# An expert's output rows scaled where they are stored and added to the residual by DMAs; VectorE's last two low pieces of the first expert unit moved up in the routing stage

## Chip, cores and metric

One core of a Trainium2 chip runs the whole program. The metric is device time in microseconds, the median of three runs; one more execution was recorded by the hardware profiler, and all rows below come from it.

## What is computed

Two layers of a decoder over 256 positions of width 1024 (batch 1). Layer 0 mixes tokens with a gated MLP and has a dense SwiGLU; layer 1 mixes with latent attention and has a SwiGLU with 8 experts, of which each position uses 2. Both mixers run beside a cross-attention into 256 memory tokens. The change touches the experts of layer 1 and the last norm:

```python
def moe_ffn(x, w_router, b_router, w_gate, w_up, w_down):
    logits = (x @ w_router).astype(jnp.float32) + b_router.astype(jnp.float32)
    top_vals, top_idx = lax.top_k(logits, TOP_K)
    weights = jax.nn.softmax(top_vals, axis=-1)
    gates = jnp.sum(jax.nn.one_hot(top_idx, N_EXPERTS, dtype=jnp.float32) * weights[..., None], axis=-2)
    out = jnp.zeros_like(x)
    for e in range(N_EXPERTS):
        out = out + gates[..., e:e + 1].astype(x.dtype) * swiglu(x, w_gate[e], w_up[e], w_down[e])
    return out
...
h = h + moe_ffn(rms_norm(h, ffn_norm[1]), ...)
return rms_norm(h, final_norm)
```

## The kernel before

**Numbers and tiles.** Every large product is made of float32 numbers split in two: a high part `hi` (ScalarE copies `raw` to it, line 1156) and a low part `lo` (VectorE subtracts, line 1606). TensorE then does three products for each block (lines 584, 585, 586: lo by hi, hi by lo, hi by hi). Weights come in units of 128 partitions by up to 3584 columns. There are three `raw` buffers and two of `hi` and `lo`, and a unit is split in four pieces. SyncE loads a unit's half into a `raw` buffer when VectorE has made the low parts of the unit that was there three units earlier (it waits on `lo_done`; helpers `load` and `expert_loads`, lines 513 and 519).

**The experts.** The program picks for every position its two experts (routing, some 490 to 510 us), then runs a loop over the experts, `ve` from 0 to 7 here (up to 16 rounds where an expert has over 128 positions). A round takes 12 units U+0 to U+11 of 896 or 1024 columns a piece: eight of gate and up weights, loaded at line 513, and four of down weights (line 519). Its 128 rows come from a table in HBM, `slots`, into which GpSimd has scattered the normalised rows by indirect DMAs (line 2322); expert 0 is fed from SBUF by a selection product instead. A round's output stays in the two PSUM banks S; at the start of the next round ScalarE copies them to `yrow` (`output_rows`, through line 1156), and SyncE stores `yrow` in block `ve` of `slots` after the loads of unit U+5 (line 524). After unit U+9's loads it fetches the next expert's rows, `xrow` (line 529). The output of the last round is never stored: it is split in high and low parts (`output_hi` on ScalarE, `output_lo` on VectorE, line 2104) and put on its positions by a selection product (`scatter`, line 1059).

**The routing stage on VectorE** is an order written out by hand: `add_tile`, `gain_tile`, `choose` (the top two of a tile's logits), `rows_lo`, `sel`, counts, and between them the four low pieces of unit U+0, by `split(U_MOE, 0, (i,))`. Pieces 0 and 1 stand inside the stage; piece 2 and piece 3 stand behind it, after each half of `gathered_lo` (line 2098, the low parts of the first expert's turned rows).

**The end.** When the outputs of the rounds before the last are stored, GpSimd gathers each position's two rows by four indirect DMAs, 512 KB each (line 2333), into `y_from[k][t]` (k is the choice, t the tile of 128 positions). VectorE multiplies each by its gate and adds it to the residual `h` (`add_rows`, line 2109), four times:

```python
            dve.wait_ge(gates_set, 1)
            dve.wait_ge(y_back, 16 * 2 * NT)
            for k in range(2):
                add_rows(k, 0)
            output_lo(0)
            add_rows(0, 1)
            output_lo(1)
            add_output(0, 0)
            add_output(0, 1)
            add_rows(1, 1)
            add_output(1, 0)
            add_output(1, 1)
```

`add_output(t, c)` (line 2116) adds the last expert's product for tile t and column half c. ScalarE squares each finished quarter (line 1585), GpSimd makes `rstd` of a tile from its two sums (lines 2339, 2341), VectorE and ScalarE scale (lines 2197, 1589), and SyncE stores the four quarters (line 546).

## Time and profile before

| | |
|---|---|
| median of 3 runs | 1008.78 us (1007.81 to 1008.89) |
| the profiled execution: its own time | 1007.8 us |
| its span, first to last instruction | 1006.0 us |
| TensorE busy | 982.1 us (98%), granted clock 0.997 of full speed |
| VectorE, ScalarE, GpSimd busy | 756.4 us (75%), 656.1 us (65%), 60.6 us (6%) |
| moved by DMAs | 287.12 MB, mean 285 GB/s |

Times are counted from the first instruction, so 992.8 is a place in the span and not a duration. In a timeline row the first number is the start, the second the busy time of the merged group, "x4" the number of instructions, and the bracket the idle time of that engine before it with what ended it. A row of a table by stretch gives the busy time of each engine with its count, then the granted clock, the mean busy share of the 16 DMA engines and what they moved. "PE" is TensorE, "DVE" VectorE, "ACT" ScalarE, "POOL" GpSimd, "SPq" SyncE's queue of DMA issues. In the profile's names `R` stands for R1, R2 and R3, in which xn, `yrow`, `xfirst` and three of the gathered tiles lie; the fourth lies in `GB` (GB1).

### The profile page before, as it was taken

The page shows a single profiled execution, that of the slowest core. Times are in us where ns is not written, and L with a number is a line of the kernel's source. Part 1 is how long each engine was busy: PE and PEld are TensorE (multiplying, and loading weights), DVE is VectorE, ACT ScalarE, POOL GpSimd, SP SyncE. Part 2 cuts the span into 40 slices and gives each one's busy share as a digit, 9 for nine tenths or more (in the row PEclk, how much of TensorE's full clock was granted, in tenths as well). Part 3 has the DMA queues.
Part 4 walks back from the last instruction along what each step waited for, and adds up shares of the span by engine and source line. Part 5 has one row for each costly group of instructions (what it writes and reads, how often), then busy time and mean ns, then how long its engine had stood idle before and what let it go on. Part 6 is the DMA issues. An engine that isn't in the chain of part 4 may idle for free.

```text
span 1006.0 us, 14574 instructions
## 1 busy us (share of the span) xinstructions
PE 982.1 (98%) x4892; PEld 829.4 (82%) x4892; DVE 756.4 (75%) x915; ACT 656.1 (65%) x886; POOL 60.6 (6%) x86
## 2 busy tenths in 40 slices
PE   8999999999999999999999999999999999999995
PEld 6987887888887998988877888888888888888883
DVE  5557665456556566666687989898998989899888
ACT  5555345452445545554596787978879787887964
POOL 1301000000000100000160000000000000000141
PEclk9999999999999999999999999999999999999998
DMA  9843689995566657233669999999999999999992
GB/s 322 237 156 128 189 250 309 289 319 156 200 202 216 220 149 190 103 124 106 219 226 400 399 384 407 378 402 371 390 374 385 406 371 401 373 387 391 381 405 101
DMA packets 150536, 287.12 MB, mean 285 GB/s; under 512 B 12769, under 2 KB 58865, under 8 KB 150498
## 3 DMA queue, kind: packets, MB, share of 16 engines
q1 hardware_dynamic: 147890, 277.64, 77.9%
q0 software_dynamic: 2608, 8.98, 2.6%
q8 instruction: 24, 0.39, 0.2%
q14 instruction: 14, 0.11, 0.0%
HBM read 269.81 MB, written 16.78 MB: 285 GB/s over the span
## 4 chain that ended last, share of the span: by engine, by line
PE 82%; DVE 8%; ACT 3%; DMA 3%; issue 2%; POOL 1%; SPq 1%; DVEq 0%; POOLq 0%; ACTq 0%
PE A L584 20%; PE A L586 20%; PE A L585 20%; PE S L584 4%; PE S L586 4%; PE S L585 4%; DVE lo L1606 3%; PE T L629 2%; DMA raw<-in_moe_w_down 1%; DMA raw<-in_moe_w_up 1%; PE T L1091 1%; ACT hi L1156 1%; PE T L664 1%; PE T L1049 1%; ACT R L1211 1%
## 5 line engine op out<-in xcount | busy, mean ns | idle before, releaser
L1606 DVE TENSOR_TENSOR lo<-raw,hi 128x1024 fp32r<-128x1024 f32 (+4 forms) x532 | 570.8, 1130 | 122.0 <-ACT hi L1156 120.0
L1156 ACT ACTIVATE hi<-raw 128x1024 fp32r<-128x1024 f32 (+4 forms) x532 | 485.2, 981 | 149.6 <-PE A L586 123.3
L584 PE MATMUL A<-lo,xT_hi 128*128 128x512 f32 x820 | 324.1, 395 | 2.5 <-DVE lo L1606 2.4
L586 PE MATMUL A<-hi,xT_hi 128*128 128x512 f32 x820 | 319.9, 390 | 0.0
L585 PE MATMUL A<-hi,xT_lo 128*128 128x512 f32 x820 | 319.6, 390 | 0.0
L584 PEld LDWEIGHTS A<-lo,xT_hi 128*128 128x128 f32 x820 | 154.3, 188 | 35.0 <-DVE lo L1606 3.2
L586 PEld LDWEIGHTS A<-hi,xT_hi 128*128 128x128 f32 x820 | 154.0, 188 | 32.3
L585 PEld LDWEIGHTS A<-hi,xT_lo 128*128 128x128 f32 x820 | 154.3, 188 | 30.2
L584 PE MATMUL S<-lo,xT_hi 128*128 128x512 f32 x224 | 89.1, 398 | 1.0 <-DVE lo L1606 1.0
L586 PE MATMUL S<-hi,xT_hi 128*128 128x512 f32 x224 | 87.5, 391 | 0.0
L585 PE MATMUL S<-hi,xT_lo 128*128 128x512 f32 x224 | 87.4, 390 | 0.0
L1156 ACT ACTIVATE xT_hi<-T 128x512 fp32r<-128x512 f32 (+1 forms) x82 | 41.6, 545 | 46.9 <-PE T L629 16.3
L584 PE MATMUL A<-lo,wk_hi 128*128 128x512 f32 (+2 forms) x152 | 56.9, 374 | 0.0
L586 PE MATMUL A<-hi,wk_hi 128*128 128x512 f32 (+2 forms) x152 | 56.3, 370 | 0.0
L585 PE MATMUL A<-hi,wk_lo 128*128 128x512 f32 (+2 forms) x152 | 56.2, 370 | 0.0
L584 PEld LDWEIGHTS S<-lo,xT_hi 128*128 128x128 f32 x224 | 42.2, 189 | 10.8 <-DVE lo L1606 2.7
L586 PEld LDWEIGHTS S<-hi,xT_hi 128*128 128x128 f32 x224 | 42.1, 188 | 8.8
L585 PEld LDWEIGHTS S<-hi,xT_lo 128*128 128x128 f32 x224 | 42.1, 188 | 8.1
L1637 DVE TENSOR_TENSOR xT_lo<-T,xT_hi 128x512 fp32r<-128x512 f32 (+1 forms) x34 | 19.6, 593 | 28.4 <-ACT xT_hi L1156 28.4
L584 PE MATMUL A<-xT_lo,hi 128*128 128x256 f32 x128 | 37.6, 294 | 0.4 <-DVE lo L1606 0.4
L629 PEld LDWEIGHTS T<-ident,R 128*128 128x128 f32 x228 | 27.4, 145 | 12.8 <-issue 4.5
L629 PE MATMUL T<-ident,R 128*128 128x128 f32 x228 | 33.4, 283 | 4.6 <-DVE R L1673 1.5
(239 smaller groups left out, 884.8 us busy)
## 6 DMA issues: line engine op xcount, KB each, us to landing
raw<-in_moe_w_down SPq DMA_DIRECT2D x64, 896.0 KB, 9.4
raw<-in_moe_w_gate SPq DMA_DIRECT2D x32, 768.0 KB, 8.0
raw<-in_moe_w_up SPq DMA_DIRECT2D x24, 768.0 KB, 7.3
raw<-in_moe_w_gate SPq DMA_DIRECT2D x16, 1024.0 KB, 6.9
raw<-in_moe_w_up SPq DMA_DIRECT2D x32, 512.0 KB, 6.8
raw<-in_moe_w_up SPq DMA_DIRECT2D x16, 1024.0 KB, 8.0
raw<-in_ff_w_gate SPq DMA_DIRECT2D x10, 1024.0 KB, 6.0
raw<-in_ff_w_up SPq DMA_DIRECT2D x10, 1024.0 KB, 7.2
```

Of the source, the lines that this page charges most:

```text
L584: nc.tensor.matmul(out, stat[0], mov[1], start=start, stop=False)
L585: nc.tensor.matmul(out, stat[1], mov[0], start=False, stop=False)
L586: return nc.tensor.matmul(out, stat[0], mov[0], start=False, stop=stop)
L629: last = nc.tensor.transpose(bank[:, i * P:(i + 1) * P], b, ident[:, :])
L664: last = nc.tensor.matmul(bank[:, i * P:(i + 1) * P], a.values[:, b, hd * P:(hd + 1) * P], PPT[:, (g - 1) % 2, at:at + P], start=b == 0, s ...
L1049: last = nc.tensor.transpose(T[j % 2][:, i * P:(i + 1) * P], xrow[:, (4 * b + i) * P:(4 * b + i + 1) * P], ident[:, :])
L1091: last = nc.tensor.transpose(T[j % 2][:, b * P:(b + 1) * P], hid[:, 4 * n + b, :], ident[:, :])
L1156: return nc.scalar.activation(out, in_, ACT.Copy)
L1211: last = nc.scalar.activation(PP[:, (g + 1) % 2, i * n:(i + 1) * n], S[gg % 2][:, i * n:(i + 1) * n], ACT.Exp, bias=nb[:, gg, i:i + 1], sc ...
L1606: nc.vector.tensor_tensor(piece(lo, SPLIT, u, i), piece(raw, RAW, u, i), piece(hi, SPLIT, u, i).bitcast(F32), ALU.subtract).then_inc(lo_do ...
L1637: nc.vector.tensor_tensor(out, T[j % 2][:, 0:n * P].rearrange("p (k s) -> p k s", k=n), hi_part.bitcast(F32), ALU.subtract).then_inc(t_fre ...
```

## The change

Four things, all in layer 1's experts:

1. **Gates as a table.** A second table in HBM, `gate_slots`, holds one gate per slot. SyncE zeroes it with one DMA, and the small tile `slot_gate` with another, ahead of the first zeroing of `slots`. After the scatter of the rows GpSimd scatters the gates by four more indirect DMAs (128 numbers each). After each round's `xrow` fetch SyncE fetches the next block's 128 gates into `slot_gate` (4 bytes to a partition), having waited once for the four scatters.
2. **Scaled where stored.** ScalarE's `output_rows` multiplies by `slot_gate` as it copies S to `yrow`, having waited for the fetch of the round before.
3. **Added by DMAs.** The four `add_rows` are gone from VectorE. GpSimd, once all four gathers have landed, issues two DMAs that add `y_from[0][t]` to `h[:, t, :]`, waits for both, and issues the two of choice 1. VectorE waits for all four (`added_in`) between `output_lo(0)` and the first `add_output`; the quarters now go c before t on VectorE and on ScalarE, and GpSimd's wait for tile 0 is for three squares in place of two.
4. **Low pieces moved.** Piece 2 of unit U+0 goes ahead of `choose(1)`, piece 3 ahead of the copy of `xfirst`.

```diff
@@ -247,6 +247,8 @@
     slot_rows = slots.rearrange("b p d -> (b p) d")
+    gate_slots = nc.dram_tensor("gate_slots", (BLOCKS * P, 1), F32, kind="Internal").ap()
+    gate_blocks = gate_slots.rearrange("(b p) o -> b p o", p=P)
@@ -333,6 +335,7 @@
         gate_row = sb("gate_row", [P, 2, NT])
+        slot_gate = sb("slot_gate", [P, 1])
         rowf = sb("rowf", [P, 2, 2, NT])
@@ -387,7 +390,8 @@
         gate_set, rows_added, tile_summed = sem("gate_set"), sem("rows_added"), sem("tile_summed")
-        gates_set = sem("gates_set")
+        gates_set, gates_in = sem("gates_set"), sem("gates_in")
+        slot_gate_in, added_in = sem("slot_gate_in"), sem("added_in")
         last_gained, last_out = sem("last_gained"), sem("last_out")
@@ -496,6 +500,11 @@
                     sp.wait_ge(zero_set, 1)
+                    if b == 0:
+                        zeros = sel[:, :].bitcast(F32)
+                        sp.dma_start(gate_slots.rearrange("(p b) o -> p (b o)", p=P), zeros[:, 0:BLOCKS]
+                                     ).then_inc(zero_in, 16)
+                        sp.dma_start(slot_gate[:, :], zeros[:, 0:1]).then_inc(slot_gate_in, 16)
                     sp.dma_start(slots[b].rearrange("p (a c) -> p a c", c=NT * P),
@@ -528,6 +537,9 @@
                                      ).then_inc(xrow_in, 16)
+                        sp.wait_ge(gates_in, 16 * 2 * NT)
+                        sp.dma_start(slot_gate[:, :], gate_blocks[bass.ds(ve + 1, 1)].rearrange("b p o -> p (b o)"),
+                                     allow_slow_non_contiguous=True).then_inc(slot_gate_in, 16)
@@ -1510,8 +1522,10 @@
                     act.wait_ge(y_stored, ve * 16 + 16)
-                act_copy(yrow[:, c * 512:(c + 1) * 512], S[(S_MOE + c) % 2][:, :]
-                         ).then_inc(s_free[(S_MOE + c) % 2], 1)
+                if c == 0:
+                    act.wait_ge(slot_gate_in, ve * 16 + 16)
+                nc.scalar.activation(yrow[:, c * 512:(c + 1) * 512], S[(S_MOE + c) % 2][:, :], ACT.Copy,
+                                     scale=slot_gate[:, 0:1]).then_inc(s_free[(S_MOE + c) % 2], 1)
@@ -1577,7 +1591,7 @@
             for n in range(4):
-                t, c = divmod(n, 2)
+                c, t = divmod(n, 2)
                 cols = slice(c * 512, (c + 1) * 512)
@@ -2067,7 +2081,7 @@
             gain_tile(1, 1)
-            split(U_MOE, 0, (1,))
+            split(U_MOE, 0, (1, 2))
             choose(1)
@@ -2086,6 +2100,7 @@
             nc.vector.tensor_tensor(r1[:, 2, :], top[:, :, 1], top[:, :, 0], ALU.subtract).then_inc(ahead_set, 1)
+            split(U_MOE, 0, (3,))
             dve.wait_ge(row_mm, 2)
@@ -2103,11 +2118,6 @@
                                         ALU.subtract).then_inc(y_lo, 1)
-
-            def add_rows(k, t):
-
-                step(nc.vector.scalar_tensor_tensor(h[:, t, :], y_from[k][t], gate_row[:, k, t:t + 1],
-                                                    h[:, t, :], ALU.mult, ALU.add))
@@ -2138,9 +2148,7 @@
             gathered_lo(T_MOE, 0, (0,))
-            split(U_MOE, 0, (2,))
             gathered_lo(T_MOE, 0, (1,))
-            split(U_MOE, 0, (3,))
             split(U_MOE + 1)
@@ -2174,17 +2182,12 @@
                     split(U + 1, ve + 1)
-            dve.wait_ge(gates_set, 1)
-            dve.wait_ge(y_back, 16 * 2 * NT)
-            for k in range(2):
-                add_rows(k, 0)
             output_lo(0)
-            add_rows(0, 1)
+            dve.wait_ge(added_in, 16 * 2 * NT)
+            add_output(0, 0)
             output_lo(1)
-            add_output(0, 0)
+            add_output(1, 0)
             add_output(0, 1)
-            add_rows(1, 1)
-            add_output(1, 0)
             add_output(1, 1)
@@ -2313,7 +2316,7 @@
             nc.gpsimd.tensor_scalar(rowf[:, 1], rowf[:, 0], r1[:, 8, 1:2], None, ALU.is_lt).then_inc(row_to_set, 1)
-            pool.wait_ge(zero_in, 16 * (BLOCKS - 1))
+            pool.wait_ge(zero_in, 16 * BLOCKS)
             pool.wait_ge(y_stored, 16)
@@ -2323,6 +2326,11 @@
             nc.gpsimd.tensor_tensor(gate_row[:, :, :], rowf[:, 1], r1[:, 5:7, :], ALU.mult).then_inc(gates_set, 1)
+            pool.wait_ge(gates_set, 1)
+            for k in range(2):
+                for t in range(NT):
+                    pool.indirect_dma_start(gate_slots, bass.IndirectOffsetOnAxis(row_to[:, k, t:t + 1], 0),
+                                            gate_row[:, k, t:t + 1], None).then_inc(gates_in, 16)
             pool.wait_ge(route_done, 1)
@@ -2333,9 +2341,15 @@
                                             ).then_inc(y_back, 16)
+            pool.wait_ge(y_back, 16 * 2 * NT)
+            for k in range(2):
+                if k:
+                    pool.wait_ge(added_in, 16 * NT)
+                for t in range(NT):
+                    pool.dma_start(h[:, t, :], y_from[k][t], accum_op=ALU.add).then_inc(added_in, 16)
             n = N_FINAL
             for t in range(NT):
-                pool.wait_ge(tile_summed, 2 * t + 2)
+                pool.wait_ge(tile_summed, t + 3)
                 step(nc.gpsimd.tensor_scalar(rstd[:, n, t:t + 1], half_sum[:, t, 0:1], half_sum[:, t, 1:2], EPS,
```

How the order moves, in three places.

VectorE, behind the routing stage and ahead of the loop over the experts, before:

```order
L2086 COPY ahead<-A 128x8 x2
L2088 TENSOR_TENSOR r<-top 128x2
L2090 COPY R<-S 128x512
L2098 TENSOR_TENSOR xT_lo<-T,xT_hi 128x512
L1606 TENSOR_TENSOR lo<-raw,hi 128x1024
L2098 TENSOR_TENSOR xT_lo<-T,xT_hi 128x512
L1606 TENSOR_TENSOR lo<-raw,hi 128x512
L1606 TENSOR_TENSOR lo<-raw,hi 128x1024 x3
L1606 TENSOR_TENSOR lo<-raw,hi 128x512
```

and with the change:

```order
L2100 COPY ahead<-A 128x8 x2
L2102 TENSOR_TENSOR r<-top 128x2
L1620 TENSOR_TENSOR lo<-raw,hi 128x512
L2105 COPY R<-S 128x512
L2113 TENSOR_TENSOR xT_lo<-T,xT_hi 128x512 x2
L1620 TENSOR_TENSOR lo<-raw,hi 128x1024 x3
L1620 TENSOR_TENSOR lo<-raw,hi 128x512
```

The piece of 512 columns (piece 3) has moved ahead of the copy of `xfirst`; the piece of 1024 (piece 2) has left this stretch and stands further up, beside piece 1. Both low parts of the turned rows now follow each other.

VectorE behind the loop, before:

```order
L2109 SCALAR_TENSOR_TENSOR h<-R,gate_row,h 128x1024 x2
L2104 TENSOR_TENSOR wk_lo<-S,wk_hi 128x512
L2109 SCALAR_TENSOR_TENSOR h<-R,gate_row,h 128x1024
L2104 TENSOR_TENSOR wk_lo<-S,wk_hi 128x512
L2116 SCALAR_TENSOR_TENSOR h<-A,gate_last,h 128x512 x2
L2109 SCALAR_TENSOR_TENSOR h<-GB,gate_row,h 128x1024
L2116 SCALAR_TENSOR_TENSOR h<-A,gate_last,h 128x512 x2
```

and with the change:

```order
L2119 TENSOR_TENSOR wk_lo<-S,wk_hi 128x512
L2126 SCALAR_TENSOR_TENSOR h<-A,gate_last,h 128x512
L2119 TENSOR_TENSOR wk_lo<-S,wk_hi 128x512
L2126 SCALAR_TENSOR_TENSOR h<-A,gate_last,h 128x512 x3
L2194 TENSOR_TENSOR R<-h,GB 128x512
```

The four rows of 1024 columns are gone, and the second `wk_lo` (`output_lo(1)`) now stands behind the first `add_output` and so behind the wait for the adding DMAs.

GpSimd from the scatter of the rows on, with the change (line 2332 and line 2349 are new):

```order
L2325 DMA slots<-R,row_to 2304x1024 x4
L2328 TENSOR_TENSOR gate_row<-rowf,r 128x4
L2332 DMA gate_slots<-gate_row,row_to 2304x1 x4
L2335 TENSOR_LOAD nround
L2335 ISA x2
L2337 ISA
L2338 TENSOR_TENSOR row_from<-row_to,row_kept 128x4
L2341 DMA R<-slots,row_from 128x1024 x3
L2341 DMA GB<-slots,row_from 128x1024
L2349 DMA h<-R 128x1024 x3
L2349 DMA h<-GB 128x1024
L2353 TENSOR_SCALAR rstd<-half_sum 128x1
```

The gate scatters stand behind the row scatters, the adding DMAs behind the gathers; nothing else moved there.

## Rows read from the trace of the kernel before

**Rows 1.** Table by stretch: PE, PEld, DVE, ACT, POOL busy, PEclk, DMA share, GB/s

```profile
508.00:513.00 5.00, 4.63 (x24) 3.46 (x23) 4.29 (x6) 3.92 (x7) 4.37 (x9) 1.00 0.01 2
521.00:527.00 6.00, 6.00 (x28) 4.94 (x27) 6.00 (x8) 5.52 (x7) 5.09 (x4) 1.00 0.93 288
527.00:534.00 7.00, 7.00 (x32) 5.82 (x31) 6.76 (x7) 4.27 (x7) 0.34 (x2) 1.00 1.03 414
600.00:700.00 100.00, 100.00 (x464) 83.55 (x463) 90.81 (x98) 81.69 (x104) 0.00 (x0) 1.00 1.03 389
```

**Rows 2.** Timeline of TensorE: where it stood still in the first round

```profile
546.95 0.50 PE L584 MATMUL A<-lo,xT_hi 128*128 128x512 f32 x1 [1.89 <-DVE lo L1606]
...
552.49 0.50 PE L584 MATMUL S<-lo,xT_hi 128*128 128x512 f32 x1 [0.48 <-DVE lo L1606]
```

**Rows 3.** Timelines of SyncE's queue (DMA issues) and of GpSimd, first round

```profile
512.60 0.37 SPq L513 DMA_DIRECT2D raw<-in_moe_w_up  x1
...
521.31 0.37 SPq L513 DMA_DIRECT2D raw<-in_moe_w_gate  x1
...
527.13 0.22 POOL L2325 TENSOR_TENSOR gate_row<-rowf,r 128x4 f32<-128x4 f32 x1
...
543.60 0.33 SPq L529 DMA_DIRECT2D R<-slots  x1
548.06 7.87 SPq L519 DMA_DIRECT2D raw<-in_moe_w_down  x4
```

**Rows 4.** Timelines of ScalarE (first row) and VectorE in and behind routing

```profile
498.31 2.00 ACT L1156 ACTIVATE hi<-raw 128x1024 fp32r<-128x1024 f32 x2
...
501.25 1.22 DVE L1606 TENSOR_TENSOR lo<-raw,hi 128x1024 fp32r<-128x1024 f32 x1
503.49 0.23 DVE L2048 SCALAR_TENSOR_TENSOR rt<-A,rstd,br 128x8 f32<-128x8 f32 x1 [1.02 <-PE A L968]
...
508.33 0.69 DVE L2090 COPY R<-S 128x512 f32<-128x512 f32 x1 [0.92 <-PE S L1031]
...
511.74 4.81 DVE L1606 TENSOR_TENSOR lo<-raw,hi 128x512 fp32r<-128x512 f32 x5
```

**Rows 5.** DMA view of 28 to 41 us, then of 98 to 104 us: issue, KB, us to landing

```profile
gbs<-in_gm_b_s POOLq DMA_DIRECT2D x1, 4.0 KB, 5.8
...
GB<-in_mem_norm POOLq DMA_DIRECT2D x1, 512.0 KB, 4.0
```

**Rows 6.** GpSimd's last gather, then the DMA view of 962 to 977 us

```profile
965.51 1.96 POOL L2333 DMA_INDIRECT GB<-slots,row_from  x1 [0.30 <-issue]
...
q0 software_dynamic: 576, 2.10, 35.4%
...
GB<-slots,row_from POOLq DMA_INDIRECT x1, 11.4
```

**Rows 7.** Timeline of the last two weight units: TensorE, ScalarE, VectorE

```profile
982.42 0.50 PE L584 MATMUL S<-lo,xT_hi 128*128 128x512 f32 x1 [0.47 <-DVE lo L1606]
...
984.67 1.79 ACT L1156 ACTIVATE hi<-raw 128x896 fp32r<-128x896 f32 x2 [0.46 <-DMA raw<-in_moe_w_down]
986.71 1.79 ACT L1156 ACTIVATE hi<-raw 128x896 fp32r<-128x896 f32 x2 [0.24 <-DMA raw<-in_moe_w_down]
...
985.66 4.13 DVE L1606 TENSOR_TENSOR lo<-raw,hi 128x896 fp32r<-128x896 f32 x4 [0.16 <-ACT hi L1156]
```

**Rows 8.** Timelines of the end: TensorE, VectorE, GpSimd

```profile
992.45 0.39 PE L586 MATMUL S<-hi,xT_hi 128*128 128x512 f32 x1
...
992.34 0.69 DVE L2104 TENSOR_TENSOR wk_lo<-S,wk_hi 128x512 fp32r<-128x512 f32 x1
...
996.51 1.27 DVE L2109 SCALAR_TENSOR_TENSOR h<-GB,gate_row,h 128x1024 f32<-128x1024 f32 x1
997.82 1.41 DVE L2116 SCALAR_TENSOR_TENSOR h<-A,gate_last,h 128x512 f32<-128x512 f32 x2
...
1002.12 0.75 DVE L2197 SCALAR_TENSOR_TENSOR R<-h,rstd,GB 128x512 f32<-128x512 f32 x1 [0.77 <-POOL rstd L2341]
...
1000.23 1.20 POOL L2339 TENSOR_SCALAR rstd<-half_sum 128x1 f32<-128x1 f32 x1 [1.61 <-ACT R L1585]
```

## The prediction

> **What bounds the kernel now.** I read the chain of waits first: TensorE carries most of it. The table by stretch [rows 1] says where that is strict. From 600 to 700 us TensorE is busy for all 100 us, and the DMAs carry 389 GB/s. In other stretches they reach 414 GB/s, so in the middle rounds TensorE alone sets the pace and a weight that comes a little earlier or later is worth nothing. That leaves three places where time can be won or lost.
>
> The first is the first round. The DMAs stand still from 508 to 513 us (2 GB/s) and run at 288 GB/s from 521 to 527, since SyncE waits to be allowed to load: the second half of unit U+3 is issued at 512.60, the first half of U+5 at 521.31 [rows 3], each when VectorE has made the low parts three units back. The bill comes at 546.95, where TensorE waits 1.89 us for low parts whose weights were late, and at 552.49, 0.48 us more [rows 2]. The second is the last two weight units, where TensorE waits again (0.47 us) and ScalarE starts each of the last halves when its DMA lands, at 984.67 and 986.71 [rows 7]: here the DMAs set the end. The third is the end itself: the last product of the experts finishes at 992.45 + 0.39 = 992.84 [rows 8], and from there to the end of the span, 1006.0, are 13.2 us of short steps, mostly VectorE's.
>
> **The low pieces moved up.** Piece 2 has had its high part since 498.31 + 2.00 = 500.31 [rows 4]. VectorE makes piece 1 at 501.25 in 1.22 us and then idles 1.02 us until the logits of tile 1. A second piece of up to 1.22 us ends at 503.69 at the latest, against 503.49 for the start of `choose(1)`; the issue overlaps by some 0.1 us, so the routing chain is **0.1 us** later, at most 0.2, at least 0. Piece 3, half a piece, fits in the 0.92 us idle before the copy of `xfirst` at 508.33. So the second half of U+3 can be issued some 4 us earlier, in the time when the DMAs stand still.
>
> What is behind it gains less. The five pieces that VectorE makes from 511.74 in 4.81 us [rows 4] become four. They can't start before their high parts, so I take U+1 and U+2 to be 1.3 us earlier, the load of U+5 with them, and from U+3 on, where ScalarE sets the pace, some 0.6 us. From 527 on the DMAs are full, so what counts is how much of the unused capacity before is recovered: (1 - 288/414) x 6 = 1.8 us between 521 and 527 [rows 1], of which loads issued 0.6 to 1.3 us earlier recover about 1. Forecast: **-1.0 us**; bounds: nothing, and both stalls, 1.89 + 0.48 = -2.4.
>
> **The gates' table.** GpSimd issues four more indirect DMAs behind 527.13 + 0.22 [rows 3]. It has nothing else to do until the gathers. They have to be in before SyncE's first fetch of gates, behind the row fetch at 543.60; the next issue there comes at 548.06 only, so 16 us and 4 more cover them. As to DMA time, the nearest row is the load of 1024 separate numbers, 5.8 us from issue to landing with other transfers beside it [rows 5]; 512 numbers are at most half of that, 2.9, in the window where the DMAs are the bound, and at least nothing. The landing holds mostly waiting, so I take 0.3. The fetches, 128 numbers each, are hidden in the middle rounds under a full TensorE; the one in the last round stands ahead of the last weights and I give it 0.1 (at most 5.8/8 = 0.7). Together **+0.4 us**, between 0 and 3.6. ScalarE's copies scaled by a column, the two zeroing DMAs and ScalarE's new wait (for a fetch issued a third of a round before) I take at nothing: TensorE's full busy time covers them.
>
> **The end without the four additions.** The four `add_rows` take 1.27 us each [rows 8]; two lie before the first `output_lo` at 992.34 and cost nothing, two lie between it and the last `add_output`, which ends at 997.82 + 1.41 = 999.23. With the change, from 992.84: the first scatter product of a tile 0.8 (estimate from four matmuls at 0.4 each, overlapped, as at the last one [rows 8]), one `add_output` 0.7, `output_lo(1)` 0.69, the second scatter 0.75, two `add_output` 1.41 give 997.2. That is 2.0 us less. GpSimd now makes tile 0's rstd right ahead of tile 1's (1.20 us for the first step at 1000.23), which may give back 0.2. What follows (square, rstd, scale, store) is the same. **-1.8 us**; bounds: -2.6 (both additions whole) and nothing.
>
> **The adding DMAs.** This is the term that decides. The last gather is issued at 965.51 and lands 11.4 us later, at 976.9 [rows 6]. GpSimd then issues two transfers of 512 KB. A plain one from GpSimd took 4.0 us from issue to landing with little beside it [rows 5], of which the data can be only about 1.3 at 400 GB/s, so the first bytes move some 2 us behind the issue, about 979.5. From there to 984.6, when the second-last half of the weights lands for ScalarE's start at 984.67, and 2 us beyond, the weights are still coming [rows 7], and both queues share the DMA engines. Their price: the four gathers, 2.10 MB, took 35.4% of the engines for 15 us, 5.3 us in all [rows 6]; two of them are 2.65. That is the cost if an adding transfer costs a copy. But it has to read `h` as well as its source; if reading is what limits, it is double, 5.3. I take the middle, 4.0. All of it fits ahead of the last weights and pushes them back. The slack there: VectorE's last four pieces end at 985.66 + 4.13 = 989.8 and three products of three matmuls (2.05 us by 0.23 each) end at 992.84, so 1.0; for the piece before, which five products follow, 0.6. So TensorE's end is 4.0 - 0.6 = **+3.4 us**; bounds 2.05 and 4.7. Nothing at all is excluded since the DMAs are full until the last weight.
>
> The second pair is issued when the first has landed. Sharing with the some 5.1 us of weights left, the first is in at 979.5 + 5.1 + 4.0 = 988.6, the second 4.0 + 3.3 (issue, first bytes, landing) later, 995.9. VectorE's first `add_output` is ready for it at 992.84 + 0.8 + 3.4 = 997.0. So `added_in` does not end last, by 1.1 us.
>
> **Sum.** +0.1 - 1.0 + 0.4 - 1.8 + 3.4 = **+1.1 us**. The profiled execution took 1007.8 us, so 1008.9 beside it; the median shown is 1008.78, 1.0 above that execution, so I predict **1009.9 us**. A measurement of this kernel tells about 0.2%, 2 us, from no change: this is inside.
>
> **Rivals.**
>
> *Two reads, half the rate.* The pair costs 5.3 us, the term 4.7, the sum -2.3 + 4.7 = +2.4: 1011.2 us. For it: the destination must be read. Against: the DMA engines' rate in these rows may be that of writing. The Trainium skill ("Collectives: The Full Stack", section "The bandwidth ceiling: the fold count and why AG ≠ RS ≠ AR") says that a transfer that adds puts two source reads on one ring and so runs at half the rate of a copy. By that rule this rival is right; no row before shows an adding transfer.
>
> *The wait takes the place of the additions.* If an adding transfer is cut small and costs three times a copy, a pair is 8.0 us. TensorE ends 7.4 later. The first pair is in at 979.5 + 5.1 + 8.0 = 992.6, the second 8.0 + 3.3 later, 1003.9, while VectorE stands ready at 993.6 + 7.4 = 1001.0 and `output_lo(1)` is queued behind that wait. Sum: -2.3 for the other terms, + 7.4 + 2.9 = +8.0, so 1016.8 us. It decides from a pair of about 5.1 us up. For it: the order puts the wait ahead of `output_lo(1)`. Against: the gathers ran at the full rate.
>
> *Faster.* The pair costs a copy (+2.05), the early half unit takes away all of the first round's stall (-2.4), the gates cost nothing: 0.1 - 2.4 - 1.8 + 2.05 = -2.05, so 1006.7 us. For it: 4 us of standing DMAs is more than the stall. Against: the later loads are not earlier by as much.
>
> **How the numbers follow.** Forecast 0.42, two reads 0.22, the wait 0.13, faster 0.23. The forecast lies within 2 us of before; two reads and the wait lie above; so 0.23 faster, 0.42 the same, 0.35 slower. The forecast's own range is 1008 to 1011. The whole range must reach both sides: down to the faster case with a full gain at the end (-2.6 instead of -1.8), 1005.9, and up to between two reads and the wait, 1015.0; beyond lie about 2 in 10.
>
> **What the profile would show.** The stall at 546.95 about 1 us shorter; the DMAs moving between 508 and 513; GpSimd's queue moving some 1 MB between 979 and 989; the last weights landing 4 us behind 986.7, seen as ScalarE waiting for them; `add_output` released by TensorE and not by a DMA; the stretch from the last expert product to the end at 11.4 us, not 13.2. I am wrong if an adding packet takes a copy's time, if `added_in` releases VectorE, or if the first stall does not shrink.

## The result, and the profile after

| | before | after |
|---|---|---|
| median of 4 runs each | 1008.32 us | 1018.65 us |
| lowest to highest | 1007.81 to 1008.89 | 1016.63 to 1020.38 |
| ratio, 95% interval | | 1.0102, 1.0081 to 1.0122 |
| the profiled execution, its span | 1007.8, 1006.0 us | 1016.63, 1014.9 us |

(A fourth run of the kernel before is in here, so its median is 1008.32 and not the 1008.78 of three.) The kernel is slower by 1.0%, 10.3 us between the medians and 8.9 us between the profiled spans. I had predicted 1009.9, range 1005.9 to 1015.0, slower with a chance of 0.35: the time lies outside the range.

Both kernels give TensorE the same 4892 matmuls in the same order, so their starts can be laid side by side. How much later each starts than in the kernel before, at eight places named by their time there:

```
                       routing  first round      middle    last weights      end
place, us before     508.1  540.1  552.5   600   975  |  982.4  989.2  992.5  span
after                +0.9   +5.2   +5.1   +5.0  +5.0  |  +4.4   +9.0   +9.1   +8.9
```

So 0.9 us come from routing, 4.1 from the first round (5.0 - 0.9), none from the middle, 4.1 from the last weights (9.1 - 5.0), and the end gives back 0.2.

**Routing.** VectorE and GpSimd in the kernel after, the timeline from 501 us:

```profile
501.22 2.35 DVE L1620 TENSOR_TENSOR lo<-raw,hi 128x1024 fp32r<-128x1024 f32 x2
504.34 0.23 DVE L2062 SCALAR_TENSOR_TENSOR rt<-A,rstd,br 128x8 f32<-128x8 f32 x1 [0.76 <-POOL rstd L2288]
...
501.51 2.15 POOL L2286 TENSOR_SCALAR rstd<-half_sum 128x1 f32<-128x1 f32 x1 [5.87 <-ACT R L1476]
503.74 0.56 POOL L2288 TENSOR_TENSOR rstd<-rstd,mhalf 128x1 f32<-128x1 f32 x1
```

`choose(1)` is 0.85 us later than in [rows 4], and not because VectorE is late: it has 0.76 us idle. It waits for GpSimd's rstd of tile 1. GpSimd's first step, one number to a partition, took 2.15 us and ended at 503.66, just when VectorE's two pieces ended (503.57).

**First round.** The table by stretch, columns as in [rows 1], of the kernel after, and under it the same two stretches of the kernel before:

```profile
534.00:538.00 4.00, 3.96 (x18) 2.96 (x16) 0.95 (x2) 1.58 (x2) 0.00 (x0) 1.00 1.04 121
538.00:544.00 6.00, 3.47 (x16) 2.40 (x16) 1.71 (x4) 1.10 (x2) 0.00 (x0) 1.00 0.93 226
544.00:550.00 6.00, 4.73 (x14) 3.79 (x15) 4.18 (x4) 4.18 (x7) 0.00 (x0) 0.72 1.06 364
```

```profile
534.00:538.00 4.00, 4.00 (x19) 3.31 (x18) 2.43 (x3) 1.90 (x3) 0.00 (x0) 1.00 1.04 402
538.00:544.00 6.00, 6.00 (x32) 5.01 (x31) 4.10 (x4) 4.57 (x7) 0.00 (x0) 1.00 1.11 358
```

The DMA engines are almost as busy as before and move far less: 121 GB/s for 402, then 226 for 358. GpSimd had issued the gates' scatters just before. Its timeline, and TensorE's stall that answers to [rows 2]:

```profile
525.94 1.66 POOL L2332 DMA_INDIRECT gate_slots<-gate_row,row_to  x1 [0.28 <-POOL gate_row L2328]
...
532.48 1.43 POOL L2332 DMA_INDIRECT gate_slots<-gate_row,row_to  x1 [0.30 <-issue]
...
545.27 0.50 PE L596 MATMUL A<-lo,xT_hi 128*128 128x512 f32 x1 [3.01 <-DVE lo L1620]
```

The stall is 3.0 us and stands 21 matmuls earlier in the program than the one of 1.89 us before. ScalarE waits 5.14 us for one load of up-weights at 542.90. After TensorE has stood still its clock is granted at 0.72 from 544 to 550, so part of that stretch runs at the lower of the two levels, 1.2 GHz in place of 2.4. Run 4 comes back to this.

The load I had looked at did come earlier: SyncE issues the second half of U+3 at 509.08, not 512.60 [rows 3].

**Last weights and end.** ScalarE, then VectorE in the kernel after, answering to [rows 7, 8]:

```profile
984.68 1.79 ACT L1168 ACTIVATE hi<-raw 128x896 fp32r<-128x896 f32 x2 [1.56 <-DMA raw<-in_moe_w_down]
986.82 1.80 ACT L1168 ACTIVATE hi<-raw 128x896 fp32r<-128x896 f32 x2 [0.34 <-DMA raw<-in_moe_w_down]
991.44 1.79 ACT L1168 ACTIVATE hi<-raw 128x896 fp32r<-128x896 f32 x2 [2.83 <-DMA raw<-in_moe_w_down]
996.15 1.79 ACT L1168 ACTIVATE hi<-raw 128x896 fp32r<-128x896 f32 x2 [2.92 <-DMA raw<-in_moe_w_down]
...
1002.02 0.60 ACT L1168 ACTIVATE wk_hi<-S 128x512 fp32r<-128x512 f32 x1 [0.76 <-PE S L598]
```

```profile
1001.29 0.69 DVE L2119 TENSOR_TENSOR wk_lo<-S,wk_hi 128x512 fp32r<-128x512 f32 x1 [2.06 <-ACT wk_hi L1168]
1003.72 0.75 DVE L2126 SCALAR_TENSOR_TENSOR h<-A,gate_last,h 128x512 f32<-128x512 f32 x1 [1.74 <-DMA h<-GB]
1004.38 0.68 DVE L2119 TENSOR_TENSOR wk_lo<-S,wk_hi 128x512 fp32r<-128x512 f32 x1
```

The last two half-units, which landed for ScalarE at 984.67 and 986.71 before, are in at 991.4 and 996.1: 9.4 us behind, of which 5.0 were there already. And at 1003.72 VectorE has waited 1.74 us for a DMA, the last of the four that add, with `output_lo(1)` queued behind that wait.

I measure the end from ScalarE's second copy of the experts' output (992.88 before; 1002.02 here) to the end of the span: 13.1 us before, 12.9 now.

### The profile page after: what moved, and what is told of

Same layout as the page of the kernel before. It is cut to its first block, busy times and chain, and to the rows that moved or that the text cites. A ratio compares the mean times of both kernels' runs of the same rounds, so it can differ in the third digit from the quotient of the medians.

```text
span 1014.9 us, 14609 instructions
## 1 busy us (share of the span) xinstructions
PE 985.7 (97%) x4892; PEld 830.4 (82%) x4892; DVE 752.0 (74%) x911; ACT 657.7 (65%) x886; POOL 70.6 (7%) x94
## 4 chain that ended last, share of the span: by engine, by line
PE 78%; DVE 6%; DMA 6%; ACT 4%; POOL 2%; issue 2%; SPq 1%; ACTq 0%; POOLq 0%; DVEq 0%
PE A L596 19%; PE A L598 19%; PE A L597 19%; PE S L596 4%; PE S L598 4%; PE S L597 4%; PE T L641 2%; DVE lo L1620 2%; DMA raw<-in_moe_w_up 2%; ACT hi L1168 2%; DMA h<-R 1%; DMA GB<-slots,row_from 1%; PE T L1103 1%; PE T L676 1%; DMA slots<-R 1%
```

## The experiments

The theory going in was that budget: GpSimd held up beside VectorE's second piece (+0.9), 4-byte writes that hold up all DMAs (+4.2), adding transfers at twice a copy's price ahead of the last weights (+4.6 from the dip at 982.4, 4.1 from the middle), and a wait that eats the gain of the end. The rivals were that the earlier load had upset the first round, and that two queues that share the engines cost the end its time whatever they carry. The shifts of TensorE in every run, read in the same way; the columns behind the bar are differences:

```
place, us before        508.1  552.5    600   975   992.5 | first  last     end,
                                                          | round  weights  us
after                    +0.9   +5.1   +5.0  +5.0   +9.1  | +4.1   +4.1    12.9
1  pieces alone          +1.1   +0.5   +0.5  +0.5   +1.2  | -0.6   +0.8    13.2
2  no adding DMAs        +0.7   +5.3   +5.2  +5.3   +4.9  | +4.6   -0.4    12.9
3  no gate scatters      +0.8   -1.5   -1.5  -1.5   +5.2  | -2.4   +6.8    12.0
4  plain copies          +1.5   +7.2   +7.1  +7.1   +9.8  | +5.6   +2.6    12.1
5  512 B rows            +0.8   +2.6   +2.6  +2.6   +7.7  | +1.8   +5.1    11.7
6  4 B, 512 B apart      +0.8   +0.6   +0.5  +0.5   +5.5  | -0.3   +4.9    12.2
7  4 B, 64 B apart       +0.6   +0.6   +0.5  +0.5   +7.2  | -0.1   +6.7    11.6
8  wait later            +3.1   +6.6   +6.6  +6.6  +10.6  | +3.5   +4.0    11.8
9  64 B, wait later      +1.1   +0.9   +0.9  +0.9   +7.7  | -0.2   +6.8    11.5
10 64 B, adds last       +0.9   -0.2   -0.3  -0.3   -0.7  | -1.2   -0.4    21.3
11 adding gathers        +0.6   +0.4   +0.3  +0.3   +4.7  | -0.3   +4.4    12.1
12 GpSimd adds, no table +1.2   +1.1   +1.1  +1.2   +5.9  |  0.0   +4.7    11.1
13 earlier add, no table +1.0   -0.3   -0.4  -0.4   +1.2  | -1.4   +1.5    12.4
14 one piece alone       +0.2   +0.5   +0.4  +0.4   -0.6  | +0.2   -1.0    13.2
```

("first round" is 600 less 508.1, "last weights" 992.5 less 975, "end" from the second copy to the end of the span.) Rows 1 and 12 to 14 are the kernel before with parts of the change or with other additions. One profiled execution each: routing alone scatters by some tenths of a us, once by 2 (row 8, where the granted clock was 0.73 from 508 to 513 us and 1.00 in the change).

### 1. The pieces alone

```diff
 (kernel before)
-            split(U_MOE, 0, (1,))
+            split(U_MOE, 0, (1, 2))
             choose(1)
...
+            split(U_MOE, 0, (3,))
             dve.wait_ge(row_mm, 2)
```

> The kernel before with the two moved low pieces alone. Theory (the budget read from the two traces: routing +0.9, gates' scatters +4.2, adding transfers +4.6, the wait eats the gain of the end): routing comes out 0.9 us later, because GpSimd's first step of tile 1's rstd stands still while VectorE makes two pieces (2.15 us instead of 1.10); the stall at 546.95 shrinks by up to 1 us since the second half of U+3 is loaded 4 us earlier; sum -0.1 to +0.9 us, so 1008.7 to 1009.7. Rival (the first round's delay comes from the earlier load, which changes the order of the loads): TensorE 4 to 5 us late after 550, 1013 to 1014 us.

Measured: 1008.20 us against 1008.84, ratio 0.9991 (0.9982 to 0.9999), 0.5 us under the expected range. The first round is not slower but 0.6 us faster than routing leaves it, and the interval just excludes no gain. The rival, 1013 us, falls.

### 2. The rows added by VectorE again

```diff
 (kernel after)
-            for k in range(2):
-                if k:
-                    pool.wait_ge(added_in, 16 * NT)
-                for t in range(NT):
-                    pool.dma_start(h[:, t, :], y_from[k][t], accum_op=ALU.add).then_inc(added_in, 16)
...
+                step(nc.vector.tensor_tensor(h[:, t, :], y_from[k][t], h[:, t, :], ALU.add))
```

> The changed kernel, its rows still scaled where stored, but added by VectorE in the places of the kernel before (plain additions), no adding DMAs. Theory: +0.9 of routing and +4.2 of the gates' scatters stay, the 4.6 on the last weights go, the end takes 13.2 us as before: 1008.8 + 5.1 = 1013.9 us, 1013.2 to 1014.5. Rival (the late last weights come from something else than the adding transfers, such as the fetch of gates ahead of them): above 1016 us.

Measured: 1013.80 us, ratio 1.0060 (1.0043 to 1.0077), the first round +4.6, the last weights -0.4. So the table of gates costs 5.6 us over the pieces alone, and the adding DMAs with all they change at the end 1018.65 - 1013.8 = 4.9.

### 3. No scatters of gates

> The changed kernel without the four scatters of gates (the table stays zero and the experts' rows of the first two choices come out as zeros: they are left out of the output); the fetches, the scaled copies and the adding DMAs stay. Theory: the DMAs keep 360 to 400 GB/s between 534 and 544 us and the first round's 4.2 us are gone: 1018.65 - 4.2 = 1014.4 us, 1013.7 to 1015. Rival (the pieces, or the zeroing of the table, cost the first round its time): 1018 us or more.

The edit takes out the loop of four `indirect_dma_start` into `gate_slots` and SyncE's wait for it. Measured: 1011.83 us, ratio 1.0033 (1.0020 to 1.0046): 6.8 us less than the change, more than the 4.2 expected and 1.9 under the range. This kernel's table stays zero, so the stored experts' rows are left out of its output; every step except the scatters is made. The stretches that stood at 121 and 226 GB/s:

```profile
534.00:538.00 4.00, 4.00 (x20) 3.30 (x19) 2.61 (x4) 1.76 (x3) 0.00 (x0) 1.00 1.05 402
538.00:544.00 6.00, 6.00 (x31) 5.13 (x30) 4.13 (x5) 5.63 (x9) 0.00 (x0) 1.00 1.11 359
```

Without the scatters the first round is 2.4 us faster than routing leaves it, so they cost not 4.1 but the gain of the pieces on top. How much that gain is, one trace doesn't tell: with both pieces moved and no scatters it is 0.6, 2.4, 0.0 and 1.4 us (rows 1, 3, 12, 13). Run 2 less run 1 makes it 5.2 in the first round and 5.6 in the time. The zeroing of the table and the fetches are still in here and cost nothing that shows.

At the end this run shows something that the change's own trace does not. Its table by stretch:

```profile
985.00:990.00 5.00, 3.46 (x16) 2.24 (x14) 2.09 (x2) 1.79 (x2) 0.05 (x1) 0.99 0.69 174
990.00:995.00 5.00, 3.20 (x8) 2.13 (x7) 2.09 (x2) 2.06 (x3) 1.65 (x2) 0.50 0.77 146
```

TensorE waited for the late weights and then ran at a granted clock of 0.50, the lower level; the products between 989 and 992.5 of the kernel before slip by 2.1 us. The last weights cost 6.8 us here for 4.1 in the change. Runs 5, 7 and 9 show the same (0.66, 0.66 and 0.50 between 995 and 1000 us; 1.7 to 2.8 us more from 989 to 992.5), runs 6 and 8 and the change itself do not (0.1). In run 11 it falls too, a little earlier in the program (0.91 from 985 to 990 us, 0.75 from 990 to 995).

### 4. The adding DMAs as plain copies

```diff
-                    pool.dma_start(h[:, t, :], y_from[k][t], accum_op=ALU.add).then_inc(added_in, 16)
+                    pool.dma_start(h[:, t, :], y_from[k][t]).then_inc(added_in, 16)
```

> The changed kernel with the four adding DMAs made plain copies of the same rows to the same places (the additions are left out of the output, h is overwritten). Theory (adding reads two operands and takes twice a copy's time): packets of that queue fall from 327 to 340 ns to about 160 to 170, the pair costs 2.65 us instead of 5.3, the last weights come 2.6 us earlier, the second pair is in before VectorE wants it, and the end gives its 1.8: 1018.65 - 4.4 = 1014.3 us, 1013.5 to 1016. Rival (two queues that share the DMA engines cost this, whatever they carry): 1018 us or more, packets above 300 ns.

Measured: 1016.24 us, ratio 1.0077 (1.0062 to 1.0092): 2.4 us less, not 4.4, and 0.2 above the range. Its first round was the worst of all (+5.6). The two stretches behind the scatters, of this run and then of run 8, which has the same packed table, differ in the granted clock:

```profile
538.00:544.00 6.00, 0.95 (x4) 0.53 (x3) 1.66 (x2) 1.58 (x2) 0.00 (x0) 0.74 1.00 214
544.00:550.00 6.00, 5.66 (x20) 4.35 (x20) 3.03 (x4) 3.25 (x4) 0.00 (x0) 0.69 0.95 294
```

```profile
538.00:544.00 6.00, 4.77 (x23) 3.43 (x23) 3.28 (x4) 1.58 (x2) 0.00 (x0) 1.00 1.01 219
544.00:550.00 6.00, 4.70 (x22) 3.55 (x21) 4.18 (x4) 4.94 (x7) 0.00 (x0) 1.00 1.02 329
```

With this table the first round costs 3.5 us where the clock stayed at 1.00 (run 8), 4.1 and 4.6 where it fell for a while (the change: 0.72 from 544 to 550; run 2: 0.82, then 0.89) and 5.6 where it fell longest. So part of this term may be the clock behind the stall, and not the late weights alone. The split is not tested: run 8 also came out of routing 2 us later, and in run 4 the DMAs were slower as well (294 GB/s from 544 to 550 for 329).

The end decides between the theories. GpSimd's queue in the DMA view while the second pair is alone, in the change (997 to 1004 us) and then here (996 to 1001 us):

```profile
q0 software_dynamic: 288, 1.05, 79.3%
...
h<-GB POOLq DMA_DIRECT2D x1, 512.0 KB, 6.6
```

```profile
q0 software_dynamic: 288, 1.05, 53.0%
...
h<-GB POOLq DMA_DIRECT2D x1, 512.0 KB, 3.7
```

The same 1.05 MB in 288 packets take 79.3% of 7 us, 5.55 us of all engines, when they add, and 53.0% of 5 us, 2.65 us, when they copy: a factor of 2.1. The last weights cost 2.6 us instead of 4.1. VectorE does not wait for a DMA, and the end takes 12.1 us:

```profile
1001.90 0.69 DVE L2119 TENSOR_TENSOR wk_lo<-S,wk_hi 128x512 fp32r<-128x512 f32 x1 [2.05 <-ACT wk_hi L1168]
1003.55 0.75 DVE L2126 SCALAR_TENSOR_TENSOR h<-A,gate_last,h 128x512 f32<-128x512 f32 x1 [0.96 <-PE A L1071]
...
1005.78 1.41 DVE L2126 SCALAR_TENSOR_TENSOR h<-A,gate_last,h 128x512 f32<-128x512 f32 x2 [0.22 <-PE A L1071]
1007.29 0.69 DVE L2194 TENSOR_TENSOR R<-h,GB 128x512 f32<-128x512 f32 x1
1008.93 1.41 DVE L2200 SCALAR_TENSOR_TENSOR R<-h,rstd,GB 128x512 f32<-128x512 f32 x2 [0.94 <-POOL rstd L2355]
```

This is the end without the four additions and without the wait: the last `add_output` ends 4.6 us behind ScalarE's second copy (1002.63), 6.35 before, so 1.8 are gained. But the rstd of both tiles now comes behind it. VectorE idles 0.94 us ahead of its first two scalings, where it went straight on before, and 0.46 for 0.77 [rows 8] ahead of the last: 0.7 go back.

### 5 to 7. What makes the scatters slow

Three tables in place of the one of 4 B per slot: 512 B per slot and written whole (with a constant, so its output is not the right one); 4 B written into rows of 512 B; 4 B written into rows of 64 B. The core of the second (the third has 16 for P):

```diff
-    gate_slots = nc.dram_tensor("gate_slots", (BLOCKS * P, 1), F32, kind="Internal").ap()
+    gate_slots = nc.dram_tensor("gate_slots", (BLOCKS * P, P), F32, kind="Internal").ap()
...
+            step(nc.gpsimd.tensor_scalar(row_far[:, :, :], rowf[:, 0], float(P), float(P * P), ALU.mult, ALU.add))
...
-                    pool.indirect_dma_start(gate_slots, bass.IndirectOffsetOnAxis(row_to[:, k, t:t + 1], 0),
+                    pool.indirect_dma_start(gate_slots.rearrange("b (o n) -> (b o) n", n=1), bass.IndirectOffsetOnAxis(row_far[:, k, t:t + 1], 0),
```

> The changed kernel with a table of 512 B for each slot, written whole by the same four scatters (rows of a constant, so what is scaled is not what the gates ask for). Theory (the four scatters hold the DMAs up because each of their 512 writes is 4 B into the same few KB): with 512 B rows a write is whole and 0.26 MB cost under 1 us; the DMAs keep above 350 GB/s between 534 and 544 us; the first round loses under 1.5 us instead of 4 to 7, the time is 1012.5 to 1014 us. Rival (the number of descriptors costs it, whatever their size): nothing changes, 1018 us or more, and the rate falls to 120 to 230 GB/s as before.

> The changed kernel with its numbers of 4 B written 512 B apart (a table 128 numbers wide, first column alone); one GpSimd step of 0.3 us more for the indices. Tells apart two readings of the slow scatters. Writes close together hit one place of the memory: spread, they cost under 1.5 us, 1012.5 to 1014 us. Writes of 4 B are slow wherever they go: 1018 us or more, the rate 120 to 230 GB/s between 534 and 544.

> As the table spread to 512 B between numbers, but 64 B (16 numbers wide). If what slows the 4 B writes is that several lie within one small block of memory (64 B or less), they cost under 1.5 us here too: 1012 to 1013.5 us. If they must lie hundreds of bytes apart, the rate between 534 and 544 us still falls below 300 GB/s and the time is 1014 to 1018.

Measured: 512 B rows 1013.80 us, ratio 1.0043 (1.0028 to 1.0058); 4 B in rows of 512 B 1012.43, ratio 1.0036 (1.0024 to 1.0048); 4 B in rows of 64 B 1012.91, ratio 1.0043 (1.0028 to 1.0059). The stretches of the second and the third:

```profile
534.00:538.00 4.00, 3.84 (x17) 2.84 (x16) 1.03 (x2) 1.58 (x2) 0.00 (x0) 1.00 1.04 398
538.00:544.00 6.00, 5.07 (x23) 3.71 (x24) 4.41 (x6) 3.82 (x5) 0.00 (x0) 1.00 1.11 361
```

```profile
534.00:538.00 4.00, 3.68 (x17) 2.71 (x15) 0.91 (x1) 1.58 (x2) 0.00 (x0) 1.00 1.04 382
538.00:544.00 6.00, 5.10 (x23) 3.78 (x24) 4.43 (x6) 3.91 (x5) 0.00 (x0) 1.00 1.11 362
```

With the same 512 writes of 4 B, by the same four DMAs, the first round is 0.1 to 1.2 us faster than routing leaves it when they lie 64 or 512 B apart (rows 6, 7, 9, 10 and 11), and 3.5 to 5.6 slower when 16 of them share 64 B; without any it is 0.0 to 2.4 faster. What spread writes still cost is not clear of the scatter between traces. Whole rows of 512 B cost more, +1.8 in their one trace, with the rate at 407 and 369 GB/s in the same two stretches. So the larger part goes with how the numbers are packed, not with their size or number. Wider spacing also makes the table larger, 9 KB at 4 B per slot and 147 KB at 64 B, and no run parts the two: whether it is neighbours in one block of 64 B, or all writes in a few KB, stays open. Which distance below 64 B would do was not tried, nor what in the memory makes it so. The Trainium skill ("DMA: Bandwidth & Descriptors", section "Specifications") says that a transfer of less than 512 B is done by reading, changing and writing back. That alone would make runs 6 and 7 as slow as the change, 1018 us, for their writes are 4 B too; the measured 1012.4 and 1012.9 decide against it as the whole cause.

### 8. The wait behind the second output_lo

```diff
             output_lo(0)
-            dve.wait_ge(added_in, 16 * 2 * NT)
-            add_output(0, 0)
             output_lo(1)
+            dve.wait_ge(added_in, 16 * 2 * NT)
+            add_output(0, 0)
```

> The changed kernel with VectorE's wait for the adding DMAs behind the second output_lo instead of ahead of it. Theory (the wait of 1.74 us holds output_lo(1) up, and the scatter of the second half behind it): output_lo(1) at 1002.7 instead of 1004.4, the end 0.7 to 1.0 us earlier: 1017.8 us. Rival (the first add_output alone decides): 1018.6, no change.

Measured: 1015.76 us, ratio 1.0071 (1.0048 to 1.0093), 2.9 less than the change, but the four runs lie between 1014.4 and 1019.3. In the trace the end takes 11.8 us for 12.9, and the wait that is left is 0.23 us. That is 1.1, a little over the 0.7 to 1.0 expected; the rest of the 2.9 I don't claim.

### 9 and 10. Closing the sum, and the additions behind the weights

> The changed kernel with both its avoidable costs taken off: numbers 64 B apart, and the wait for the adding DMAs behind the second output_lo. If the parts add up as read so far (pieces -0.6, scatters spread and fetches about +0.7, adding DMAs on the last weights +4.6, the end -1.1): 1008.8 + 3.6 = 1012.4 us less the share of the wait, 1011.5 to 1012.5. Rival (the parts overlap, something else of the change costs): above 1013.5 us.

> As the one with numbers 64 B apart and the later wait, but GpSimd issues the adding DMAs only when ScalarE has made the high part of the last weights' second-last piece, so that all weights are in. Theory (the 4.6 us are bytes ahead of the last weights, nothing else): the last weights land when they do in the kernel before, TensorE's last expert product ends 4 to 5 us earlier; but the two pairs, one behind the other, take 6.6 + 7.1 us from there (about 988 + 13.7 = 1001.7) and end 5 to 6 us behind the moment VectorE is ready: 1011.5 to 1012.5 us, about the same. Rival (the adding packets hold up more than their own time, so that moved behind the weights they cost less): below 1010.5 us.

The second of them adds, ahead of GpSimd's wait for the gathers:

```diff
+            pool.wait_ge(hi_done, n_pieces(U_MOE + 11, rounds - 1) + 3)
+            step(nc.gpsimd.tensor_tensor(r1[:, 8, 0:1], r1[:, 7, 1:2], r1[:, 7, 1:2], ALU.mult))
             pool.wait_ge(y_back, 16 * 2 * NT)
```

Measured: 1013.76 us, ratio 1.0051 (1.0034 to 1.0068), and 1016.19, ratio 1.0081 (1.0060 to 1.0101). The first is 1.3 us above the range I expected and 0.3 above the line set for the rival: with 6.8 us on the last weights it is among those whose clock fell, to 0.50. The second misses by 3.7. The weights are back in their place (TensorE 0.7 us early), but VectorE stands:

```profile
1003.19 2.73 DVE L2127 SCALAR_TENSOR_TENSOR h<-A,gate_last,h 128x512 f32<-128x512 f32 x4 [9.71 <-DMA h<-GB]
```

I had the first pair issued at 988.0 (it was 988.49), gave the pairs 13.7 us (14.7) and mis-added what follows. Two pairs in a row, alone, are a chain of 14.7 us, of which the moving itself is 2 x 5.55. Ahead of the weights they cost bytes, behind them their whole latency, which is worse.

### 11. Gathers that add

```diff
-                    pool.indirect_dma_start(y_from[k][t], None, slot_rows,
-                                            bass.IndirectOffsetOnAxis(row_from[:, k, t:t + 1], 0)
-                                            ).then_inc(y_back, 16)
+                    if k and not t:
+                        pool.wait_ge(added_in, 16 * NT)
+                    pool.indirect_dma_start(h[:, t, :], None, slot_rows,
+                                            bass.IndirectOffsetOnAxis(row_from[:, k, t:t + 1], 0),
+                                            compute_op=ALU.add).then_inc(added_in, 16)
```

> The changed kernel with the spread table, and with the gathers themselves adding to h (the first choice's two, then, when they are in, the second choice's two) in place of gathers and adding DMAs. Theory (an adding packet costs twice a copy's, and only half as many bytes move as with gathers and adding DMAs): the queue's share falls from 10.6 + 5.3 us of engine time to 10.6 in all; the last weights land 2.6 us later than in the kernel before instead of 4.6 to 7, no wait for the sums at the end, which takes 12.0 us instead of 13.1: about 1008.9 + 2.6 - 1.1 + 0.0 = 1010 to 1011 us. Rival (adding rows of an indirect DMA costs more than twice a copy): above 1012.4 us.

Measured: 1011.24 us, ratio 1.0026 (1.0006 to 1.0046). Of the versions with a table of gates it is the fastest, and still no faster than the kernel before. The DMA view of the stretch with its four gathers (958 to 991 us), and of the kernel before with its four (958 to 978):

```profile
q0 software_dynamic: 576, 2.10, 31.9%
```

```profile
q0 software_dynamic: 576, 2.10, 26.6%
```

10.5 us of engine time for 2.10 MB, against 5.3: twice again. My expectation had these 10.6 right and then put the last weights 2.6 late; the difference to the kernel before is 5.3, and they came 4.4 us late, in a trace in which the clock fell too (see run 3). The time lies 0.2 above the expected range.

### Two ways to take work from the end without DMAs

These are rows 12 and 13 of the table, and one piece alone is row 14. GpSimd scales and adds tile 1's rows (four operations), on the kernel before with the two pieces moved:

> The kernel before with the two moved low pieces and tile 1's rows scaled and added by GpSimd (four operations of 128x1024, from about 978 us, when the gathers are in) in place of two of VectorE's additions. Theory: GpSimd waits while VectorE makes pieces, so each takes 1 to 3 us and they are in by 990; both additions leave the stretch behind the last expert product: 1008.2 - 2.5 = 1005.7 us. Rival (GpSimd's operations hold VectorE's pieces up, or are themselves held up to the last piece and end behind 997): 1008 us or more.

Measured: 1010.00 us, ratio 1.0012 (1.0002 to 1.0021), so 1.8 slower than without. GpSimd and VectorE in that kernel:

```profile
978.45 3.15 POOL L2336 TENSOR_SCALAR R<-R,gate_row 128x1024 f32<-128x1024 f32 x1 [10.89 <-DMA GB<-slots,row_from]
981.70 3.04 POOL L2336 TENSOR_SCALAR GB<-GB,gate_row 128x1024 f32<-128x1024 f32 x1
984.82 2.97 POOL L2337 TENSOR_TENSOR h<-R,h 128x1024 f32<-128x1024 f32 x1
987.86 3.11 POOL L2338 TENSOR_TENSOR h<-GB,h 128x1024 f32<-128x1024 f32 x1
...
983.43 12.50 DVE L1606 TENSOR_TENSOR lo<-raw,hi 128x896 fp32r<-128x896 f32 x8 [0.35 <-ACT hi L1156]
```

The theory had GpSimd's times right (3.0 to 3.15 us each, in by 991), and the rival still won. VectorE's eight pieces took 1.56 us each in place of 1.03 (4.13 / 4 in [rows 7]): the last weights came 4.7 us late where the pieces alone have 0.8, and the end gained 2.1 (11.1 us for 13.2).

VectorE's addition of the first choice to tile 1, ahead of its last eight pieces:

```diff
                 with dve.If(ve < rounds - 1):
+                    split(U + 10, ve)
+                    split(U + 11, ve)
...
+            add_rows(0, 1)
+            split(U + 10, rounds - 1)
+            split(U + 11, rounds - 1)
             for k in range(2):
                 add_rows(k, 0)
             output_lo(0)
-            add_rows(0, 1)
             output_lo(1)
```

> The kernel before with the two moved low pieces, and in the last round VectorE's addition of the first choice's rows to tile 1 ahead of its last eight pieces (from about 981 us, where it idled 0.5 us and the gathers are in since 977) instead of between the two output_lo; the pieces of U+10 and U+11 stand behind the loop for that. Theory: the last pieces end 0.6 to 0.8 us later, of which TensorE has slack for most, and VectorE, which is busy without a break from the last expert product to the last add_output, loses 1.28 us there: 1008.2 - 0.8 = 1007.4 us, 1006.8 to 1007.8. Rival (the last pieces have no slack: what the addition takes there it takes in full): 1008.2 to 1008.8.

Measured: 1007.59 us against 1008.85, ratio 0.9987 (0.9978 to 0.9996). It beats both kernels, by 0.13% over the one before; its lead over the pieces alone is within their intervals. The trace shows both halves of the theory: the end takes 12.4 us for 13.2, and the last weights come 1.5 us late for 0.8.

One piece alone, moved to behind `choose(1)`:

> The kernel before with piece 2 alone moved, to just ahead of the copy of xfirst (1.22 us of work in 0.92 us of idle time) and piece 3 left behind the second gathered_lo. Theory (routing came 0.6 to 0.9 us late because GpSimd's first step of rstd waits for VectorE's two pieces): routing is as before up to 507 us, the GpSimd step takes 1.1 us, xfirst is 0.3 us late, U+3's second half is issued about 1 us earlier: 1008.0 us, within 0.5 of the two moved pieces. Rival (the gain of the moved pieces needs the 4 us earlier load): 1008.8 us.

Measured: 1008.34 us against 1008.85, ratio 0.9999 (0.9989 to 1.0008); by time it can't be told from either. The mechanism can. GpSimd's first step of rstd:

```profile
501.69 1.09 POOL L2283 TENSOR_SCALAR rstd<-half_sum 128x1 f32<-128x1 f32 x1 [5.87 <-ACT R L1464]
```

1.09 us with one piece beside it, 2.15 with two, and TensorE at 508.1 is 0.2 us late where every run with both pieces is 0.6 to 1.5 us late (and one 3.1).

## Why the prediction was wrong, by its own steps

**The low pieces, +0.1 and -1.0.** Together -0.9; alone they gave -0.6 in the time. The sum held, partly by luck: the parts were not as told. "The issue overlaps by some 0.1 us" left out GpSimd: I asked when VectorE would be free and not who works beside it. The Trainium skill ("SBUF — State Buffer", section "SBUF: two separate sides") has the rule that I should have weighed: a VectorE operation with two inputs in SBUF and a GpSimd operation that reads SBUF exclude each other for the whole instruction. The trace agrees, 1.09 us with one piece and 2.15 with two. Routing was 0.9 late. The first round gave 0.0 to 2.4 us back in four traces, where I had 1.0. In the changed kernel none of the gain was left, for the next term lay on the same stretch.

**The gates' table, +0.4, between 0 and 3.6. This is the step that failed.** It cost 5.6 us over the pieces alone (run 2 less run 1), outside its own bounds. That the scatters land in time was right, and that the fetches and the zeroing are hidden too (runs 2 and 3 have them; the last weights of run 2 are 0.4 early). What was wrong is the price of the DMA time. I took as upper bound a load of 1024 separate numbers, "512 numbers are at most half of that". That row is a read into SBUF; the change writes 4 B numbers side by side into HBM, and what it costs is not their own packets' time but that of the weights beside them, which fell to 121 GB/s. Nothing in the trace before shows such a write, so a row that was only near in size could not bound it. Runs 5 to 7 show that the packing sets most of it. This step alone puts the time outside the range: by estimate 1018.65 - (5.6 - 0.4) = 1013.4 us would have been inside, and the runs with spread numbers (1012.4 to 1013.8 us with the weights behind the adding DMAs) are.

**The adding DMAs, +3.4, between 2.05 and 4.7.** +4.1 in the change's trace, inside its bounds, between my 3.4 and the rival's 4.7. Of the seven traces with these DMAs ahead of the last weights (4.0 to 6.8 us) five lie above 4.7. The price of a pair was mine to choose between 2.65 and 5.3, and I took 4.0; alone it measures 5.55. The rival "Two reads, half the rate" was right in the rate; no run here shows that the second read is the reason. The Trainium skill ("Collectives: The Full Stack", section "The bandwidth ceiling: the fold count and why AG ≠ RS ≠ AR") states half a copy's rate for the reducing step of a collective, and the trace agrees for these DMAs, 5.55 us for 2.65. The first bytes moved later than I had them: the rate in the DMA view falls from about 420 to 300 GB/s at 986, 4 us behind the issue at 982.1 where I had taken 2. What no term held is the clock: where TensorE waited for such weights it was granted 0.50 for a while afterwards in four of the seven traces, and the last weights then cost 5.1 to 6.8 (4.0 to 4.9 in the others). The changed kernel's profiled execution escaped it at the end; I can't show whether its three longer runs (mean granted clock 0.990 to 0.993, for 0.994) did.

**The end, -1.8.** Run 4 shows it whole: 1.8 us are gained up to the last `add_output` and 0.7 given back behind it, where I had forecast 0.2, because both tiles' rstd now come behind the last `add_output`. In the change the wait took a further 0.8 to 0.9, so that 0.2 was left.

**"`added_in` does not end last, by 1.1 us."** Wrong by 2.8: it ended last by 1.74. The second pair landed at 997.10 + 6.6 = 1003.7. The rival "The wait takes the place of the additions" put its threshold at a pair of about 5.1 us, and the pair is 5.55, so it held in kind, with 1.7 us of wait and not 2.9. Its total of 1016.8 is close to the time, but for another reason: it has 7.4 us on the last weights and nothing in the first round.

**The sum.** By the trace +0.9 + 4.1 + 4.1 - 0.2 = 8.9. I had put these terms at +1.1. Of the 7.8 between, 4.7 are the first round's (the gates, and the gain of the pieces that they hid), 1.6 the end's, 0.8 routing's and 0.7 the adding DMAs'. The medians are 10.3 apart and not 8.9 because the profiled execution of the change was the fastest of its four, 2.0 under its median, and that of the kernel before 0.5 under its own. The medians of the runs give the same picture: -0.6 for the pieces, 5.6 for the table, where I had 0.4, and 4.9 for the adding DMAs with the changed end, where I had 3.4 - 1.8 = 1.6.

## What to carry to other kernels

Bound a new transfer by a row of the same direction, size and closeness, or give it no upper bound, and ask what it does to the transfers beside it. Small scattered writes into a packed table can cost more than the kilobytes they hold: spread them (64 B apart was enough here; whole rows of 512 B did no better). An adding DMA counts as two copies, on the engines that still bring the last weights. Before filling an idle gap of one engine, look who else starts work in it.

## What was not expected of the hardware

- 512 writes of 4 B, 16 of them to 64 B, came with a fall of all DMAs together from 402 to 121 GB/s for 4 us and from 358 to 226 for 6 more; 64 B apart, 382 and 362.
- An adding DMA between tiles takes 5.55 us of all 16 engines for 1.05 MB, a copy 2.65; an adding gather 10.5 us for 2.10 MB, a plain one 5.3.
- GpSimd's step on one number per partition lasted until VectorE's float32 pieces beside it had ended (1.09 us with one, 2.15 with two), and its operations of 128x1024 beside them took 3.0 to 3.15 us each while the pieces went from 1.03 to 1.56.
- After a wait of TensorE at the end the granted clock was 0.50 for a while in some executions and 1.00 in others of nearly the same program; where it fell in the last products it cost 1.7 to 2.8 us. After the stall of the first round it was 0.69 to 0.89 over 6 us in three traces and 1.00 in the fourth.
